# Sample forgetting attention: keys transposed in 32x32 blocks by VectorE, scores in sixteen TensorE tiles

## What is computed

```python
def fox_sample(q, k_new, v_new, lf_new, k_past, v_past, lf_past):
    ...
    s_past = jnp.einsum('bqhd,bkhd->bhqk', q, k_past).astype(jnp.float32) * scale
    s_past = s_past + suf[:, :, None, :] + c_new[:, :, :, None]
    ...
    p = jax.nn.softmax(jnp.concatenate([s_past, s_new], axis=-1), axis=-1).astype(v_new.dtype)
    n_past = k_past.shape[1]
    out = (jnp.einsum('bhqk,bkhd->bqhd', p[..., :n_past], v_past)
           + jnp.einsum('bhqk,bkhd->bqhd', p[..., n_past:], v_new))
```

## Time and profile before

| | |
|---|---|
| median of 3 runs | 3358.1 us (3355.78 to 3361.2) |
| the profiled execution, first to last instruction | 3354.0 us |
| TensorE busy | 3234.5 us (96%) |
| VectorE / ScalarE / GpSimd busy | 1297.8 us (39%) / 1096.0 us (33%) / 511.4 us (15%) |
| DMA over the whole span | 515.69 MB, mean 154 GB/s |
| first and last transpose of a key page (line 2203) | 649.1 us and 1183.5 us |

### The profile page before, as it was taken

One profiled execution on the slowest core, in us unless ns is written; L12 is line 12 of the kernel. 1 busy time (PEld: TensorE's weight loads), 2 busy tenths in 40 slices (PEclk: granted clock), 3 DMA queues, 4 the chain that ended last, 5 costly groups with the idle time before them and its releaser, 6 DMA issues. The chain is left out here.

```text
span 3354.0 us, 51636 instructions
## 1 busy us (share of the span) xinstructions
PE 3234.5 (96%) x19705; PEld 2772.9 (83%) x19705; DVE 1297.8 (39%) x2582; ACT 1096.0 (33%) x2157; POOL 511.4 (15%) x769
## 2 busy tenths in 40 slices
PE   7999999999999998999999999997999999996999
PEld 7999999777777777878888887886999888785887
DVE  4331223232333215545555554333222246655332
ACT  3112232122322225455666653222223244112211
POOL 3310000101111112244433330000000012211000
PEclk9999999999999999989999999999999999997999
DMA  5444533579899964443332225432333544756431
GB/s 158 126 135 144 163 110 120 162 229 304 298 325 310 305 183 141 128 126 89 92 92 85 89 73 169 132 104 82 121 108 102 172 127 145 228 162 210 132 110 56
DMA packets 409588, 515.69 MB, mean 154 GB/s; under 512 B 50855, under 2 KB 298216, under 8 KB 407919
## 3 DMA queue, kind: packets, MB, share of 16 engines
q1 hardware_dynamic: 386503, 444.68, 42.7%
q0 software_dynamic: 22848, 67.78, 6.2%
HBM read 388.50 MB, written 124.22 MB: 153 GB/s over the span
## 5 line engine op out<-in xcount | busy, mean ns | idle before, releaser
L420 ACT ACTIVATE z_st_p<-bank 128x512 f32<-128x512 f32 (+3 forms) x322 | 166.8, 518 | 643.5 <-PE bank L393 641.7
L393 PE MATMUL bank<-h00hi,w_hi_p 128*128 128x352 f32 x960 | 317.4, 331 | 3.9 <-DVE h00lo L1165 3.5
L1829 PE MATMUL bank<-w_hi_o,b_hi_o 128*128 128x512 f32 x782 | 305.6, 391 | 14.0 <-DVE w_lo_o L1755 14.0
L393 PE MATMUL bank<-h00hi,w_lo_p 128*128 128x352 f32 x960 | 309.3, 322 | 0.0
L393 PE MATMUL bank<-h00lo,w_hi_p 128*128 128x352 f32 x960 | 309.1, 322 | 0.0
L1830 PE MATMUL bank<-w_hi_o,b_lo_o 128*128 128x512 f32 x782 | 305.4, 390 | 0.0
L1831 PE MATMUL bank<-w_lo_o,b_hi_o 128*128 128x512 f32 x782 | 305.3, 390 | 0.0
L835 PE MATMUL bank<-pT_fa,v_fa 128*128 128x256 f32 x1092 | 272.0, 369 | 4.4 <-issue 2.4
L393 PE MATMUL bank<-h01hi,w_hi_p 128*128 128x512 f32 x640 | 266.7, 417 | 0.0
L336 DVE CAST w_hi_p<-w_raw_p 128x1024 fp32r<-128x1024 f32 x128 | 89.0, 696 | 422.1 <-PE bank L393 392.9
L393 PE MATMUL bank<-h01hi,w_lo_p 128*128 128x512 f32 x640 | 251.3, 393 | 0.0
(11 more groups left out here) (341 smaller groups left out, 6862.6 us busy)
## 6 DMA issues: line engine op xcount, KB each, us to landing
k_raw_sf<-in_cache_fox_k SPq DMA_DIRECT2D x128, 512.0 KB, 5.3
v_raw_sf<-in_cache_fox_v POOLq DMA_DIRECT2D x128, 512.0 KB, 6.0
z<-z_st_p SPq DMA_DIRECT2D x112, 512.0 KB
w_raw_p<-in_fox_w_in SPq DMA_DIRECT2D x80, 512.0 KB, 5.2
b_raw_o<-bT SPq DMA_DIRECT2D x32, 768.0 KB, 6.2
w_raw_p<-in_pool_w_in SPq DMA_DIRECT2D x48, 512.0 KB, 5.1
out<-tok_p SPq DMA_DIRECT2D x64, 256.0 KB, 4.2
w_raw_o<-z SPq DMA_DIRECT2D x62, 256.0 KB, 2.8
```

What stands on the lines that cost most here:

```text
L393: last = nc.tensor.matmul(bank[:, 0:width], wt[:, u, k, :], h[:, k, at0:at0 + width], start=(m == 0), stop=(m == MM - 1))
L420: nc.scalar.activation(z_st[0:rows_t, t % 2, at0:at0 + width], bank[0:rows_t, 0:width], tiles[t][2]).then_inc(z_read, 1)
L1829: nc.tensor.matmul(bank(t, half)[:, :], bh, w_hi, start=(k == 0), stop=False)
```

## The change

1. **Keys.** The PE transposes and their two copies go. DVE transposes a page in one instruction, from `k_raw` to `kT`, in 32x32 blocks: element (token 32y+k, column 32c+i) goes to (partition 32y+i, column 32c+k). So the partition group y holds the tokens 32y to 32y+31 of the page, and a head's 128 dimensions lie in four blocks x, one after the other along the row.
2. **Scores.** They are formed after every fourth page (`quad`). For two heads g of a column group, four blocks x, four partition groups y and four column groups j there is one matmul with 32 rows and 32 columns of queries against 128 keys (32 of each of four pages): 128 matmuls, in an order that goes through the 16 tiles (y, j) of the array before it comes back to the first. Each y has its own bank (four banks, `S_BANKS`).
3. **Queries.** The scores with the cached keys need them in partition groups: `q4` is loaded by four more DMAs, `qx4` (two sequences at a time) is filled by ACT. The old `qx`, `q_raw` and `kn_raw` now lie in the second half of `kT` and serve only the scores of the new tokens.
4. **Bias and maximum.** Four DVE operations of 128 columns for four pages in place of two of 256 columns.
5. **Buffers.** Key buffers go from four to three (`KR = 3`); the output bank of the products from two to one, so a sequence's first product waits until the sequence before has been scaled out (`o_d`).

```diff
-    KR, VR = 4, 4
+    KR, VR, Q, B = 3, 4, 4, 32
-    T_BANKS, S_BANK, O_BANKS, M_BANK = banks[0:2], banks[2], banks[3:5], banks[5]
+    S_BANKS, O_BANK, M_BANK = banks[0:4], banks[4], banks[5]
-    kT = c.sb("kT", [P, 2, FH, 2 * P])
+    kT = c.sb("kT", [P, 2, Q, FH, Q, B])
+                for n in range(Q):
+                    sp.dma_start(q4[B * n:B * (n + 1), :, :], zT[0:D, cols].rearrange("(x k) n -> k x n", k=B)).then_inc(q4_in, 16)
...
-            for x in ([i] if i < KR else [s + KR - 1] if s + KR - 1 < NPG else []):
+            for x in ([i] if i < KR else [s + KR - 1] if 1 <= s < NPG - KR + 1 else []):
                 if x >= KR:
-                    sp.wait_ge(kt_d, 2 * (x - KR + 1))
+                    sp.wait_ge(kt_d, x - KR + 1)
...
-            if 0 <= s < NPG:
-                pe.wait_ge(k_in[s % KR], 16 * (s // KR + 1))
-                for n, copied in enumerate((ka_d, kv_d)):
-                    if s:
-                        pe.wait_ge(copied, s)
-                    for h in range(4):
-                        last = nc.tensor.transpose(T_BANKS[n][:, h * P:(h + 1) * P], k_raw[:, s % KR, (4 * n + h) * P:(4 * n + h + 1) * P], ident[:, :])
-                    last.then_inc(kt_d, 1)
-            if pair(s) is not None:
+            if quad(s) is not None:
+                b, n = quad(s)
+                G = PAGES // Q * b + n
+                pe.wait_ge(kt_d, Q * (G + 1))
+                pe.wait_ge(q4_d, 2 * (b + 1))
                 if G:
-                    pe.wait_ge(sc_d, G)
-                for g in range(2):
-                    for j in range(JT):
-                        h = 2 * j + g
-                        last = nc.tensor.matmul(S_BANK[CT * j:CT * (j + 1), 0:2 * P], qx[:, b, h, :], kT[:, G % 2, h, :], start=(g == 0), stop=(g == 1))
+                    pe.wait_ge(sc_d, Q * G)
+                for m in range(2 * Q):
+                    g, x = divmod(m, Q)
+                    for y in range(Q):
+                        at = slice(B * y, B * (y + 1))
+                        for j in range(JT):
+                            h = 2 * j + g
+                            last = nc.tensor.matmul(S_BANKS[y][CT * j:CT * (j + 1), 0:P], qx4[at, b % 2, h, x, :], kT[at, G % 2, :, h, x, :],
+                                                    start=(m == 0), stop=(m == 2 * Q - 1))
                 last.then_inc(s_done, 1)
...
             if 0 <= s < NPG:
-                dve.wait_ge(kt_d, 2 * s + 2)
-                if s % 2 == 0 and s >= 4:
-                    dve.wait_ge(s_done, s // 2 - 1)
-                nc.vector.tensor_copy(kT[:, s // 2 % 2, 4:8, s % 2 * P:(s % 2 + 1) * P], T_BANKS[1][:, :].rearrange("p (h n) -> p h n", h=4)).then_inc(kv_d, 1)
+                G = s // Q
+                dve.wait_ge(k_in[s % KR], 16 * (s // KR + 1))
+                if s % Q == 0 and G:
+                    dve.wait_ge(new_d if G == 1 else s_done, 1 if G == 1 else G - 1)
+                nc.vector.transpose(kT[:, G % 2, s % Q, :, :, :].rearrange("p h x k -> p (h x k)"), k_raw[:, s % KR, :]).then_inc(kt_d, 1)
...
+                for y in range(Q):
+                    dst = part[:, y, :, :]
+                    nc.vector.tensor_tensor_reduce(out=dst, in0=S_BANKS[y][:, 0:P].rearrange("p (x k) -> p x k", x=Q), in1=dst, scale=1.0,
+                                                   scalar=LOWEST, op0=ALU.add, op1=ALU.max, accum_out=mx[:, b % 2, Q * n + y:Q * n + y + 1]).then_inc(sc_d, 1)
```

More of the change, by code:

```diff
@@ L2029, in sample_fox @@
     ident = const["ident"]
-    JT, CT, NP2, NV = 4, 32, PAGES // 2, PAGES + 1
-    KR, VR = 4, 4
+    JT, CT, NV = 4, 32, PAGES + 1
+    KR, VR, Q, B = 3, 4, 4, 32
     W = PAGES * P
     NG = (NV + 3) // 4
-    T_BANKS, S_BANK, O_BANKS, M_BANK = banks[0:2], banks[2], banks[3:5], banks[5]
+    S_BANKS, O_BANK, M_BANK = banks[0:4], banks[4], banks[5]
     c = Core(nc, stack, "sf", room)
-    q_raw, g_all, out_all, kn_raw = (c.sb(n, [P, FH, NS]) for n in ("q_raw", "gate", "out_all", "kn_raw"))
-    qx = c.sb("qx", [P, DB, FH, CT])
+    g_all, out_all = (c.sb(n, [P, FH, NS]) for n in ("gate", "out_all"))
+    q4, qx4 = c.sb("q4", [P, FH * Q, NS]), c.sb("qx4", [P, 2, FH, Q, CT])
     k_raw, v_raw = c.sb("k_raw", [P, KR, D]), c.sb("v_raw", [P, VR, D])
-    kT = c.sb("kT", [P, 2, FH, 2 * P])
+    kT = c.sb("kT", [P, 2, Q, FH, Q, B])
+    start = kT[:, 1, :, :, :, :].rearrange("p y h x k -> p (y h x k)")
+    qx = start[:, 0:DB * FH * CT].rearrange("p (b h r) -> p b h r", b=DB, h=FH)
+    q_raw, kn_raw = (start[:, DB * FH * CT + n * FH * NS:DB * FH * CT + (n + 1) * FH * NS].rearrange("p (h n) -> p h n", h=FH) for n in range(2))
     sc = c.sb("sc", [P, 2, NV * P])
@@ L2052, in sample_fox @@
     suf_in = [c.sem(f"suffix_loaded{u}") for u in range(2)]
-    kt_d, ka_d, kv_d, s_done, sc_d = (c.sem(n) for n in ("k_transposed", "kT_front_copied", "kT_back_copied", "scores_done", "scores_biased"))
+    kt_d, q4_in, q4_d, s_done, sc_d = (c.sem(n) for n in ("k_transposed", "queries_spread", "queries_split", "scores_done", "scores_biased"))
     nm_d, p_d, rr_d = (c.sem(n) for n in ("maximum_ready", "exp_done", "inverse_ready"))
@@ L2069, in batch, with quad @@
         return b if rest == 0 and 0 <= b < DB else None
-    def pair(s):
-        g = s // 2 - 1
-        return divmod(g, NP2) if s % 2 == 0 and 0 <= g < DB * NP2 else None
+    def quad(s):
+        g = s // Q - 1
+        return divmod(g, PAGES // Q) if s % Q == 0 and 0 <= g < DB * PAGES // Q else None
     def turn(s):
@@ L2218, in pe @@
                 y = NV * b + p
-                if p == 0 and b >= 2:
-                    pe.wait_ge(o_d, b - 1)
+                if p == 0 and b:
+                    pe.wait_ge(o_d, b)
                 if p % 4 == 0:
@@ L2224, in pe @@
                 for j in range(JT):
-                    last = nc.tensor.matmul(O_BANKS[b % 2][CT * j:CT * (j + 1), 0:2 * P], pT[:, p, CT * j:CT * (j + 1)],
+                    last = nc.tensor.matmul(O_BANK[CT * j:CT * (j + 1), 0:2 * P], pT[:, p, CT * j:CT * (j + 1)],
                                             v_raw[:, y % VR, 2 * P * j:2 * P * (j + 1)], start=(p == 0), stop=(p == PAGES))
@@ L2239, in act @@
                                          ACT.Copy, scale=SCALE).then_inc(qx_d, 1)
-            if 0 <= s < NPG:
-                act.wait_ge(kt_d, 2 * s + 1)
-                if s % 2 == 0 and s >= 4:
-                    act.wait_ge(s_done, s // 2 - 1)
-                nc.scalar.copy(kT[:, s // 2 % 2, 0:4, s % 2 * P:(s % 2 + 1) * P], T_BANKS[0][:, :].rearrange("p (h n) -> p h n", h=4)).then_inc(ka_d, 1)
+            for b in ([0, 1] if i == 1 else [batch(s, -13)]):
+                if b is not None and (b >= 2 or i == 1):
+                    if b == 0:
+                        act.wait_ge(q4_in, 16 * Q)
+                    if b >= 2:
+                        act.wait_ge(s_done, PAGES // Q * (b - 1))
+                    for g in range(2):
+                        nc.scalar.activation(qx4[:, b % 2, :, :, :].rearrange("p (j g) x r -> p g j x r", g=2)[:, g, :, :, TN * g:TN * (g + 1)],
+                                             q4[:, :, :].rearrange("p (j g x) n -> p g j x n", g=2, x=Q)[:, g, :, :, TN * b:TN * (b + 1)],
+                                             ACT.Copy, scale=SCALE).then_inc(q4_d, 1)
             if turn(s) is not None:
@@ L2271, in dve @@
             if 0 <= s < NPG:
-                dve.wait_ge(kt_d, 2 * s + 2)
-                if s % 2 == 0 and s >= 4:
-                    dve.wait_ge(s_done, s // 2 - 1)
-                nc.vector.tensor_copy(kT[:, s // 2 % 2, 4:8, s % 2 * P:(s % 2 + 1) * P], T_BANKS[1][:, :].rearrange("p (h n) -> p h n", h=4)).then_inc(kv_d, 1)
-            if pair(s) is not None:
-                b, n = pair(s)
-                G = NP2 * b + n
+                G = s // Q
[3 more added lines that the diff above has]
+                nc.vector.transpose(kT[:, G % 2, s % Q, :, :, :].rearrange("p h x k -> p (h x k)"), k_raw[:, s % KR, :]).then_inc(kt_d, 1)
+            if quad(s) is not None:
+                b, n = quad(s)
+                G = PAGES // Q * b + n
                 dve.wait_ge(s_done, G + 1)
```

25 lines of the change are left out of this document (10 added, 15 removed).

## The result

The changed kernel takes 3497.3 us (median of 4 runs, 3492.9 to 3497.7) where the kernel before takes 3356.9 us (4 runs, 3352.6 to 3361.2): a ratio of 1.0417, 95% interval 1.0402 to 1.0432. The forecast was 3318 us and faster; it was wrong in sign, and the time lies outside the range.

What follows compares the result with a forecast made beforehand. PE was taken to set the pace, with DMA nearly full at 0.93. PE's gain, capped by DMA at 40 us, gave 3354.0 - 40 = 3314 us for the profiled execution, 3318 us for the median; range 3265 to 3372 us.

Steps and rivals of the forecast that it cites:

- The reading of the kernel before: Key-page stretch, 649 to 1184 us: PE sets the pace, buffers are full ahead of it, DMA needs 0.93 in the middle.
- I expect the same of sixteen and take 2.3 us: New scores of four pages: sixteen tiles run side by side, 2.3 us against 5.2 us before, gaining 2.9 us.
- both bounds: New scores of four pages: 1.8 us if all 16 tiles stream at once, 2.5 us by PE's instruction pace.
- The second bound: New scores: PE's pace for small instructions, 0.0098 us a record from the new tokens' scores, so 2.5 us for four pages.
- The 16 tiles do not run at once: Rival, new scores: four pages cost 6.4 to 7.0 us on PE; +38 to +58 us, 3396 to 3416 us; chance 0.12.
- over 5.2 says the second rival: Profile sign: score groups taking over 5.2 us to the next matmul's start would mean the 16 tiles don't run at once.
- The Trainium skill's rule in that step: New scores: matmul starts never under about 25 ns apart, so four pages cost 6.4 us and the change loses 38 us.
- What DMA leaves: Key-page stretch: PE's gain counts only until DMA is full; 40 us together, 52 us with DMA at 1.0.
- the first rival: DMA in the attention: not full at a share of 1, so PE's 93 us come through; 3280 us; chance 0.15.
- DVE's price per page: DVE transposes of key pages: 1.2 us each, adding 0.5 us a page, 65 us in all, hidden behind PE and DMA.
- Late scores: Scores late by 1 to 2 us when DVE's weight split precedes the transpose; 10 to 20 us of PE, covered by DMA.
- the start: Start: extra DMAs and clearing lose 2 to 6 us, against fewer first-page stops; -2 to +4 us, 0 in the sum.

Runs made afterwards that it cites:

- run 13: Kernel before the change, with each key and value page after the first four loading only 16 of its 128 rows: 3355.1 us, ratio 1.0003.
- run 8: Changed kernel with only 64 of each group's 128 score matmuls, in one run, leaving out half of the score work: 3283.8 us, ratio 0.9783.
- Run 4: Kernel before the change, with 128 added matmuls of 4 columns, results unread, ahead of every second pair's scores: 3621.6 us, ratio 1.0785.
- run 14: Changed kernel with scores in four parts at successive page steps, later pages loading 16 of 128 rows: 3331.8 us, ratio 0.9929.
- run 3: Changed kernel with only 16 of each group's 128 score matmuls, leaving out seven eighths of the score work: 3275.2 us, ratio 0.9751.
- run 7: The kernel of run 5 with each of the 128 DVE transposes done twice: 3381.7 us, ratio 1.0069.
- run 6: The kernel of run 5 with four key and three value buffers in place of three and four: 3393.0 us, ratio 1.0112.
- run 10: The kernel of run 5 with products one step later, between the halves, and four key and three value buffers: 3378.9 us, ratio 1.0070.
- four parts: Changed kernel with each group's 128 score matmuls as 32 at each of four successive page steps, softmax and products three steps later: 3354.6 us, ratio 0.9996.
- run 5: Changed kernel with each group's score matmuls in two halves of 64, two page steps apart, what follows two steps later: 3393.4 us, ratio 1.0112.

## Why the prediction was wrong

**The reading of the kernel before held.** PE sets its pace and the pages are loaded ahead: run 13 shows it outright, with DMA at 0.33 and the time unchanged.

**The step that failed is the cost of a group, "I expect the same of sixteen and take 2.3 us".** It was 7.55 us. Two things are in the difference. First, the two groups that did not stop took 3.5 us and the halves of run 8 1.94 us each: 13 to 15 ns a record, not 7 to 10. That is above both bounds from which I took 2.3, and it would still have been a gain of 1.5 to 1.9 us a group, 50 to 60 us in all, since the work replaced took 173.9/32 = 5.4 us (5.2 in the prediction). Second, 107.4/32 = 3.4 us of stop a group, and the lower clock, which costs the groups 20 us, 0.6 a group (40 us of their work ran at 1.2 GHz). The second bound came from a row of 128 records in 1.25 us; with their weight loads those are 256 instructions, one block. The row showed the pace inside a block, and I stretched it to two. Run 4 measures the error: with matmuls of 4 columns as in that row, a burst of 512 instructions takes 6.1 us instead of 2.5.

**A second term was missing: what the stop does to its neighbours.** Products and projection, which the change does not touch, took 71.5 us more, 56 of them by the clock. The prediction has no line for them.

**The rival with the right sign, "The 16 tiles do not run at once", had the right threshold and the wrong mechanism.** "The change loses from the point where a group of 128 takes more than 5.2 us" holds. But its partition groups do overlap: at 7.0 us a group no arrangement of the same matmuls could have got to 128.3 us in all, 4.0 us a group, as run 14 did. Its time, 3396 to 3416 us, was 80 to 100 us short, since it knew nothing of the stops and the clock. What the profile would have shown against it stands in the prediction as "over 5.2 says the second rival"; that sign alone would have led to the wrong cause, and only the row with the stop inside the group tells them apart.

**The Trainium skill's rule in that step**, a floor of 25 ns between starts (the Trainium skill, "TensorE: Matmul & The Clock Gate", the section on the 56 ns gap), pointed at the right side for another reason: in sixteen tiles the starts of records were 13 to 15 ns apart wherever PE did not stop, so the floor does not hold here. The page of the Trainium skill that bears on the cause I had not weighed: "Runtime: NRT & Kernel Launch", section "Instruction fetch mechanics". It says that PE's instructions are refilled in blocks of 256 while the ones before run, and calls the cost mostly hidden. The blocks agree with the count of packets above; that it is hidden holds at the earlier trace rows, with 256 instructions in 1.25 us, and not for runs of 512. That page of the Trainium skill gives PE room for 2048 instructions and in another sentence speaks of two blocks; the stops at the second edge within a run, in 30 of 32 groups, fit the two blocks, and the two groups whose packet came early went on to the third.

**What DMA leaves** was too little. I allowed 40 us, 52 us with the DMA engines at a share of 1.0. With the score work mostly gone the gain was 80 us (run 3) and with half of it 72 us (run 8), at a share of 0.98 and 342 to 345 GB/s against 0.93 and 309. The share rose by 5% and the bytes by 11%: a part of the share is waiting, as the first rival had it. But this limit was never reached by a kernel that does all of the work.

**DVE, ACT, buffers.** DVE's price per page was right, and it is hidden (run 7). A fourth key buffer at the values' expense gained nothing (run 6) and in another order cost 11 us (run 10); what three key buffers cost by themselves no run shows. Late scores were 10 us, of the 10 to 20 forecast, but that is luck: 8.3 us are the wait of the first group, which the forecast has under the start, and the mechanism that it priced shows once, with 2.1 us.

**What stays open.** Run 14 against run 13: its scores are 45 us cheaper by starts than transposes and scores (128.3 against 173.5), its time 23 us. The projection takes 17 us more by starts (492.1 against 475.0): 5 are waits (8.4 us for the first four key pages, against 4.4 for the first page), 8 are the last projection matmul ahead of each piece of side work (0.285 us in the mean against 0.248), and 4 are spread over the others. Why that last matmul takes longer is not shown. No version beat the kernel before with its pages loaded in full; four parts equals it.

## What to carry to other kernels

Before you replace few large instructions by many small ones, count instructions per microsecond of the engine and the longest run of short ones, with weight loads: PE's blocks hold 256, and PE passes an edge only when the packet for it has landed. Here packets never started less than 3.3 us apart, and runs of 512 short instructions, which came from one edge to the next in 1 to 2 us, stopped at the second in 30 of 32 groups of 32x32 tiles and in all 32 bursts of 128x32 ones. The price of a small instruction read from a short burst holds only for bursts as short as that. If the work must be small, spread it between long matmuls: the same 128 matmuls, 32 times over, cost 143 us more in one run each than in four; and heavy loads on the DMA engines, which cost the kernel before nothing, made each such stop longer (3.5 against 1.6 us).

## What was not expected of the hardware

- Two packets of PE's instruction queue (q8) never started less than 3.3 us apart, in any of the 16 traces; in the kernel before never under 8.7 us. In the groups of the changed kernel PE came from one edge of a block to the next in as little as 1.6 us.
- A refill queues with the other loads: with 247 GB/s over all queues in the middle of the attention the stops in the scores averaged 3.5 us, with 89 GB/s 1.6 us (107.4 us in 31 stops, 46.1 in 29), and the packet's own duration did not change.
- In a stop of PE from 807.1 to 811.1 us (run 5) its granted clock fell to 1.2 GHz, at 809.8 us, and rose again at 816.6 us, after 5.5 us of work. In the changed kernel that cost unchanged work 56 us and the groups 20, beside 107 us of stops in the groups.
- Sixteen 32x32 tiles took a record of 128 columns every 13 to 15 ns while instructions were there.
